# A two-layer encoder trunk: the order of a square, a sum, a root and a product in the last two token tiles of the gated recurrence

## The chip, the cores and the metric

The kernel runs on one core of one Trainium2 chip. The metric is the device time of one execution in microseconds (us); the time of a kernel is the median of its runs. The engines are named as in the profile: PE is TensorE (its weight loads are PEld), DVE is VectorE, ACT is ScalarE, POOL is GpSimd, SP issues most of the transfers. SBUF is the on-chip working memory, PSUM the eight banks that PE writes its products to.

## The reference, cut to what matters

Each of the two layers adds three branches to h: a mixer (latent attention, and two gated linear recurrences, GLA and HGRN2), a cross-attention on a memory, and a gated MLP. There are 512 tokens of 1024 numbers. The change lies in the end of the two recurrences:

```python
def gla_mixer(...):
    o = chunked_gated_recurrence(q * GLA_DK ** -0.5, k, v, log_alpha)   # 4 heads of 64
    o = rms_norm(o, out_norm) * jax.nn.silu(r)
def hgrn2_mixer(...):
    o = chunked_gated_recurrence(silu(q) * HGRN_DK ** -0.5, one_minus_f, i, log_f)
    o = rms_norm(o, out_norm) * jax.nn.silu(g)
...
h = h + jnp.concatenate([y_a, y_b, y_c], axis=-1) @ w_mix_out[l]
```

So for every token and head the 64 outputs are squared and summed, multiplied by the inverse root of their mean, then by a gate, and the 512 numbers of both recurrences go as columns 512 to 1023 into the product with `w_mix_out`.

## The kernel before, in words

The program is written by hand for each engine: every engine has its own instruction stream, runs it in the order in which it is written, and waits on semaphores (`wait_ge`, counted through `past(layer, ...)`). Nothing reorders it. Tokens are in NT = 4 tiles of 128, and the loop below is over them. Both layers run the same code.

The end of the recurrence, called here the tail, goes through five steps for each token tile n (numbered 0 to 3 as in the code; the third and the fourth tile are n = 2 and n = 3):

1. PE makes the outputs of the 8 heads in PSUM bank `O_BANKS[n]` = 2, 3, 0, 1 (lines 1169 and 1176), 128 tokens by 512 columns, and marks `o_mm`.
2. ACT squares the bank into `o_sq[:, n % 2]`, two buffers (line 1653).
3. DVE sums the squares by head (`squares`, line 2225, marks `o_ss`).
4. ACT takes the inverse root of the 8 means with a logarithm and an exponential (`inverse_rms`, lines 1378 and 1379, marks `o_r`), 128x8 numbers.
5. DVE multiplies the bank with the roots into `o_tok` in SBUF (`gated`, line 2231, marks `o_evac`): the root product.

Then comes the gate `sg_tok`. For tiles 0 to 2 POOL multiplies (`recurrences`, line 641, marks `o_done`), for tile 3 DVE does (line 2241, marks `last_o_done`); both inputs of these products, `o_tok` and `sg_tok`, lie in SBUF.

PE turns `o_tok` with 16 transposes into four banks (`turn_o`, line 1187). Their order is: tile 0 and 1 into banks 2 and 3 (4 transposes), tile 2 into banks 2 and 3, tiles 0 to 2 into bank 0, tiles 0 to 2 into bank 1 (8 that follow one behind the other), then tile 3 into banks 0, 1, 2, 3 (the last 4, which wait for `last_o_done`). Behind them on PE stand 6 matmuls of an operand that has long been there (`mix_units(MIX_UNITS["y"])`, with `ya_hi`, `ya_lo`), then the products with `yb_hi` and `yb_lo`, the two halves of the turned tiles, which ACT (line 1660) and DVE (line 2244) make out of the banks.

Weights come as slabs of 128x1024 numbers. Each is split into a rounded half `w_hi` (ACT, line 1370) and a rest `w_lo` (POOL, line 690: `raw` minus `w_hi`, both inputs in SBUF, one output to SBUF). POOL's stream has the tail's three gate products between the rest of slab ("mix", 0, 1) and that of ("mix", 0, 2): line 690 follows the gate product of tile 2 directly, it waits only for its `w_hi`, and its slab is the one that the first products with `yb_hi` use.

```python
POOL: for n in range(NT - 1): wait o_evac >= n + 1; o_tok[:, n] *= sg_tok[:, n]     # L641
      then, of the next slab:  wait hi_split;  w_lo = raw - w_hi                       # L690
DVE:  after gated(NT - 1):     wait sg_scaled, o_evac; o_tok[:, NT-1] *= sg_tok[:, NT-1]   # L2241
```

Of the kernel before, what the change touches and what calls it, by code (L numbers as in the profile page):

```python
# [27 lines left out]
def build_trunk(nc, A, out):  # L28
# [15 lines left out]
    NT, KD, MT = SEQ // P, D // P, NM // P  # L44
# [5 lines left out]
    GDK, GDV = A["gla_w_gate"].shape[2] // NH, A["gla_out_norm"].shape[1]  # L50
# [154 lines left out]
    for g in range(len(LG)):  # L205
        for c in range(LG[g]):
            ffn_in_slabs(g, c, LG_FIRST[g] + c)
        for q, (_, b) in enumerate(PRODUCTS):
            for s, nk in pair_slabs(g):
                slab(("out", g, q, s), nk, HALF, (b, g, s))  # L210
# [3 lines left out]
    def slab_of(layer, name):  # L214
        return layer * NS + slab_at[name]
# [9 lines left out]
    for gi, (_, _, src) in enumerate(flat):  # L225
        if callable(src):
            ring_of[gi] = len(in_ring)
            in_ring.append(gi)
        if gi in dma_los:
            continue  # L230
        if callable(src) and gi not in border:
            pool_los[gi] = len(pool_los) + 1
        else:
            out_los[gi] = len(out_los) + 1
# [9 lines left out]
    with ExitStack() as ctx:  # L244

        def sb(name, shape, dt=f32):
            return ctx.enter_context(nc.sbuf_tensor(name, shape, dt))
# [22 lines left out]
        small = sb("small", [P, 636])  # L270
# [112 lines left out]
        S = {n: ctx.enter_context(nc.semaphore(n)) for n in names}  # L383
# [38 lines left out]
        R_QK, R_O, R_KR = 260, 420, 548  # L422
# [53 lines left out]
        def past(layer, name):  # L476

            return layer * PER_LAYER[name]
# [15 lines left out]
        with nc.Block() as block:  # L494
# [833 lines left out]
            def _(act_):  # L1328
# [20 lines left out]
                for layer in range(DEPTH):  # L1349
                    def split_through(i):  # L1350

                        while nsplit[0] <= min(i, len(flat) - 1):
                            k = nsplit[0]
                            nk, cols, src = flat[k]
                            n = nk * cols
                            if k in ring_of:
                                whole = raw[ring_of[k] % RAW][:, 0:n]
                                act_.wait_ge(raw_in[ring_of[k] % RAW], arrivals[k])
                            else:
                                name, g, s = src  # L1360
                                whole = b_slab(k // NS, name, s, nk)
                                if name in T_AT:
                                    act_.wait_ge(S["t_done"], t_count(k // NS, g, name, s))
                                else:
                                    act_.wait_ge(b_in[name], b_loads(k // NS, g))
                            if k >= SPLIT:
                                act_.wait_ge(*released[k - SPLIT])
                            if k in dma_los:
                                act_.activation(w_lo[k % SPLIT][:, 0:n], whole, ACT.Copy, scale=-1.0).then_inc(S["negated"], 1)  # L1369
                            act_.activation(w_hi[k % SPLIT][:, 0:n], whole, ACT.Copy).then_inc(S["hi_split"], 1)  # L1370
                            nsplit[0] += 1

                    def ahead(name):

                        split_through(slab_of(layer, name) + SPLIT - 1)

                    def inverse_rms(dst, tmp, ss, n, done):
                        link(act_.activation(tmp, ss, ACT.Ln, bias=eps_c[:, 0:1], scale=1.0 / n))
                        act_.activation(dst, tmp, ACT.Exp, scale=-0.5).then_inc(done, 1)
# [83 lines left out]
                    if layer == 0:  # L1463
                        c = FIRST_K * P
# [77 lines left out]
                    for t in range(NT):  # L1542
                        c = R_QK + 4 * t
# [3 lines left out]
                    for t in range(NT):  # L1547
# [6 lines left out]
                        c = R_QK + 4 * (NT + t)  # L1554
# [90 lines left out]
                        act_.activation(k_hat[:, f, 0:NT - 1], pb[f][:, 0:(NT - 1) * P].rearrange("p (n q) -> p n q", n=NT - 1), ACT.Copy).then_inc(S["khat_evac"], 1)  # L1645
                    act_.preload_act_table_set(LOG_EXP)
                    ahead(("mix", 0, 1))
                    for n in range(NT + 1):
                        if n < NT:
                            act_.wait_ge(S["o_mm"], past(layer, "o_mm") + n + 1)  # L1650
                            if n > 1:
                                act_.wait_ge(S["o_ss"], past(layer, "o_ss") + n - 1)
                            act_.activation(o_sq[:, n % 2, :], pb[O_BANKS[n]][:, :], ACT.Square).then_inc(S["o_sq_done"], 1)
                        if n:
                            c = R_O + 8 * (n - 1)
                            act_.wait_ge(S["o_ss"], past(layer, "o_ss") + n)
                            inverse_rms(small[:, c + 64:c + 72], small[:, c + 32:c + 40], small[:, c:c + 8], GDV, S["o_r"])
                    for c in range(4):
                        act_.wait_ge(S["yT_mm"], past(layer, "yT_mm") + c + 1)
                        act_.activation(yb_hi[:, c, :], pb[c][:, :], ACT.Copy).then_inc(S["yT_hi"], 1)  # L1660
# [45 lines left out]
                    for t in range(NT):  # L1706
                        c = R_CQ + 4 * t
# [40 lines left out]
                    for g in range(len(LG)):  # L1748
                        for c in range(LG[g]):
                            n = LG_FIRST[g] + c  # L1750
# [28 lines left out]
            def _(dve):  # L1779
# [50 lines left out]
                for layer in range(DEPTH):  # L1830
# [377 lines left out]
                    for n in range(NT - 1):  # L2208
# [4 lines left out]
                        if n:  # L2213
                            for f in range(3):
                                c = slice(0, 256) if f == 0 else slice(P + f * P, 2 * P + f * P)
# [7 lines left out]
                    def squares(n):  # L2223
                        dve.wait_ge(S["o_sq_done"], past(layer, "o_sq_done") + n + 1)
                        dve.reduce_sum(small[:, R_O + 8 * n:R_O + 8 * n + 8], o_sq[:, n % 2, :].rearrange("p (h x) -> p h x", x=64), AX.X
                                       ).then_inc(S["o_ss"], 1)

                    def gated(n):
                        c = R_O + 8 * n + 64
                        dve.wait_ge(S["o_r"], past(layer, "o_r") + n + 1)  # L2230
                        dve.tensor_tensor(o_tok[:, n, :].rearrange("p (h x) -> p h x", x=64), pb[O_BANKS[n]][:, :].rearrange("p (h x) -> p h x", x=64),
                                          small[:, c:c + 8].unsqueeze(2).to_broadcast([P, 8, 64]), ALU.mult).then_inc(S["o_evac"], 1)

                    squares(0)
                    for n in range(NT):
                        if n + 1 < NT:
                            squares(n + 1)
                        gated(n)
                    dve.wait_ge(S["sg_scaled"], past(layer, "sg_scaled") + NT)
                    dve.wait_ge(S["o_evac"], past(layer, "o_evac") + NT)  # L2240
                    dve.tensor_tensor(o_tok[:, NT - 1, :], o_tok[:, NT - 1, :], sg_tok[:, NT - 1, :], ALU.mult).then_inc(S["last_o_done"], 1)  # L2241
# [22 lines left out]
                    for t in range(NT):  # L2264
                        c = R_CQ + 4 * t
# [34 lines left out]
                    for g in range(len(LG)):  # L2300
# [6 lines left out]
                        for c in range(LG[g]):  # L2307
                            n = LG_FIRST[g] + c
# [33 lines left out]
```

## Time and profile before

| what | value |
|---|---|
| median of 3 runs | 1375.46 us (1374.12 to 1375.72) |
| the profiled execution's own time | 1374.74 us |
| its span (first to last instruction) | 1373.0 us |
| mean granted TensorE clock | 1.000 |
| busy: PE, PEld, DVE, ACT, POOL | 99%, 82%, 70%, 51%, 38% |
| the tail of the first layer | about 206 to 219 us of the span |
| the tail of the second layer | about 886 to 900 us |

The span is the part of the execution that the profile shows; 1.74 us lie around it. Times within it count from its first instruction. A busy share is an average over the whole span; what a change in the tail is worth is read from the tail, by what each engine waits for there.

### The profile page before, as it was taken

What the parts mean: (1) busy time and instruction counts of PE and PEld (TensorE: products, weight loads), DVE (VectorE), ACT (ScalarE), POOL (GpSimd) and SP (SyncE); (2) the same over time, 40 slices, a digit from 0 to 9 for tenths busy, and PEclk for the clock granted to TensorE, in tenths of its full rate; (3) what the DMA queues carried; (4) which work ended last, traced back from release to release, by engine and by line L of the source; (5) the groups of instructions that cost most, each with busy time, mean ns of one, the idle gap of its engine ahead of it and who ended that gap; (6) DMA issues with size and microseconds to landing.
All of it is one profiled execution on the core that took longest, in us unless ns stands there. A gap on an engine that the chain in (4) does not pass through costs nothing.

```text
span 1373.0 us, 19396 instructions
## 1 busy us (share of the span) xinstructions
PE 1357.8 (99%) x7551; PEld 1128.6 (82%) x7551; DVE 958.8 (70%) x1380; ACT 705.6 (51%) x1170; POOL 516.0 (38%) x327
## 2 busy tenths in 40 slices
PE   8999999999999999999999999999999999999999
PEld 6888778887879988998988887788778888888887
DVE  4583773665889569857985657836658895797587
ACT  6747483665444344434466465835754433434333
POOL 5745665642430222032036456655335203220420
PEclk9999999999999999999999999999999999999999
DMA  6332112331471475066133220133325706741641
GB/s 181 100 91 74 31 47 79 122 108 49 150 200 47 144 194 138 17 177 154 22 92 93 86 77 16 48 97 118 92 62 169 198 17 177 191 107 39 189 95 61
DMA packets 180923, 142.58 MB, mean 104 GB/s; under 512 B 15169, under 2 KB 153184, under 8 KB 180832
## 3 DMA queue, kind: packets, MB, share of 16 engines
q1 hardware_dynamic: 175664, 124.55, 30.3%
q0 software_dynamic: 4608, 16.78, 6.4%
q8 instruction: 60, 0.98, 0.3%
q14 instruction: 31, 0.25, 0.1%
q10 hardware_dynamic: 560, 0.01, 0.0%
HBM read 122.44 MB, written 2.10 MB: 91 GB/s over the span
## 4 chain that ended last, share of the span: by engine, by line
PE 92%; DVE 4%; ACT 2%; DMA 1%; issue 1%; POOL 0%; SPq 0%; DVEq 0%; POOLq 0%
PE bank L770 27%; PE bank L772 27%; PE bank L771 27%; PE bank L944 2%; PE bank L1101 1%; PE bank L1102 1%; PE bank L1087 1%; PE bank L932 1%; DMA w_lo<-raw 1%; PE bank L1254 1%; PE bank L1169 1%; DVE scores_h L2181 1%; DMA x_tok<-in_x 1%; PE bank L1011 1%; DVE Q L2164 0%
## 5 line engine op out<-in xcount | busy, mean ns | idle before, releaser
L690 POOL TENSOR_TENSOR w_lo<-raw,w_hi 128x1024 fp32r<-128x1024 f32 (+3 forms) x148 | 360.0, 2437 | 642.0 <-ACT w_hi L1370 640.4
L770 PE MATMUL bank<-x_hi,w_hi 128*128 128x512 f32 x944 | 371.8, 394 | 4.0 <-DMA w_lo<-raw 1.9
L771 PE MATMUL bank<-x_lo,w_hi 128*128 128x512 f32 x944 | 367.7, 390 | 0.0
L772 PE MATMUL bank<-x_hi,w_lo 128*128 128x512 f32 x944 | 367.7, 389 | 0.0
L1370 ACT ACTIVATE w_hi<-raw 128x1024 fp32r<-128x1024 f32 (+2 forms) x181 | 189.4, 1047 | 125.5 <-PE bank L772 124.8
L770 PEld LDWEIGHTS bank<-x_hi,w_hi 128*128 128x128 f32 x944 | 177.2, 188 | 47.5 <-issue 8.0
L771 PEld LDWEIGHTS bank<-x_lo,w_hi 128*128 128x128 f32 x944 | 177.3, 188 | 37.2 <-issue 1.4
L772 PEld LDWEIGHTS bank<-x_hi,w_lo 128*128 128x128 f32 x944 | 177.2, 188 | 37.0
L771 PE MATMUL bank<-p_lo,w_hi 128*128 128x256 f32 x308 | 87.3, 283 | 0.0
L772 PE MATMUL bank<-p_hi,w_lo 128*128 128x256 f32 x308 | 87.3, 283 | 0.0
L770 PE MATMUL bank<-p_hi,w_hi 128*128 128x256 f32 x308 | 87.2, 283 | 0.0
L1729 ACT ACTIVATE conv<-conv 128x512 f32<-128x512 f32 x44 | 27.9, 633 | 113.8 <-DVE conv L2292 113.8
L770 PE MATMUL bank<-w_hi,x_hi 128*128 128x512 f32 (+1 forms) x192 | 77.3, 403 | 0.0
L772 PE MATMUL bank<-w_hi,x_lo 128*128 128x512 f32 (+1 forms) x192 | 74.0, 385 | 0.0
L771 PE MATMUL bank<-w_lo,x_hi 128*128 128x512 f32 (+1 forms) x192 | 73.8, 384 | 0.0
L1833 DVE SCALAR_TENSOR_TENSOR x_lo<-h,gains_all,x_hi 128x512 fp32r<-128x512 f32 x40 | 39.7, 1015 | 45.6 <-ACT x_hi L1390 44.8
L680 POOL DMA_DIRECT2D w_lo<-raw x32 | 28.8, 900 | 98.6 <-ACT w_lo L1369 98.6
L1369 ACT ACTIVATE w_lo<-raw 128x1024 fp32r<-128x1024 f32 x32 | 33.7, 1054 | 59.8 <-PE bank L772 59.8
L2296 DVE TENSOR_TENSOR act<-bank,r_bc 128x512 f32<-128x512 f32 x44 | 30.3, 688 | 42.9 <-PE bank L772 42.7
L770 PE MATMUL bank<-w_hi,p_hi 128*128 128x512 f32 x154 | 60.1, 390 | 0.0
L772 PE MATMUL bank<-w_hi,p_lo 128*128 128x512 f32 x154 | 60.0, 389 | 0.0
L771 PE MATMUL bank<-w_lo,p_hi 128*128 128x512 f32 x154 | 59.9, 389 | 0.0
(351 smaller groups left out, 2766.0 us busy)
## 6 DMA issues: line engine op xcount, KB each, us to landing
raw<-in_w_ffn_in SPq DMA_DIRECT2D x88, 512.0 KB, 4.2
w_lo<-raw POOLq DMA_DIRECT2D x32, 512.0 KB, 4.8
raw<-in_w_in SPq DMA_DIRECT2D x27, 512.0 KB, 3.8
raw<-in_w_mix_out SPq DMA_DIRECT2D x16, 512.0 KB, 3.9
raw<-in_w_ca_kv SPq DMA_DIRECT2D x32, 256.0 KB, 3.4
b_y<-in_w_ffn_out SPq DMA_DIRECT2D x10, 512.0 KB, 5.8
b_x<-in_w_ffn_out SPq DMA_DIRECT2D x10, 512.0 KB, 5.3
b_z<-in_w_ffn_out SPq DMA_DIRECT2D x10, 512.0 KB, 5.5
```

What stands on the lines that cost most here:

```text
L680: pool.dma_start(w_lo[gi % SPLIT][:, 0:n], raw[ring_of[gi] % RAW][:, 0:n], accum_op=ALU.add).then_inc(lo_in[dma_los[gi][0]], 16)
L690: pool.tensor_tensor(w_lo[gi % SPLIT][:, c0:n], whole[:, c0:n], w_hi[gi % SPLIT][:, c0:n].bitcast(f32), ALU.subtract).then_inc(S["lo_split ...
L770: pe.matmul(o, ah, bh, start=first, stop=False, skip_group_check=shared_bank)
L771: pe.matmul(o, ah, bl, start=False, stop=False, skip_group_check=shared_bank)
L772: mm = pe.matmul(o, al, bh, start=False, stop=last, skip_group_check=shared_bank)
L932: mm = pe.transpose(pb[b][:, c:c + P], pr[j % FLIGHT][:, c:c + P], ident[:, :])
L944: mm = pe.matmul(pb[b][:, q0:SEQ], values(n, hd), pT[hd % len(pT)][:, n, q0:SEQ], start=(n == 0), stop=(n == n_blocks - 1))
L1369: act_.activation(w_lo[k % SPLIT][:, 0:n], whole, ACT.Copy, scale=-1.0).then_inc(S["negated"], 1)
L1370: act_.activation(w_hi[k % SPLIT][:, 0:n], whole, ACT.Copy).then_inc(S["hi_split"], 1)
L1729: act_.activation(conv[n % 2][:, :], conv[n % 2][:, :], ACT.Silu).then_inc(S["silu_done"], 1)
L1833: dve.scalar_tensor_tensor(x_lo[:, k, :], h[:, k, :], gain_of(layer + w // 3, name, k), x_hi[:, k, :].bitcast(f32), ALU.mult, ALU.subtract ...
L2296: link(dve.tensor_tensor(act[n % 2][:, :], pb[b + 1][:, :], r_bc[:, :], ALU.mult))
```

## The change

In each layer ACT takes the roots of tile 2 before it squares tile 3, and DVE makes the root product of tile 2 before it sums the squares of tile 3. No instruction is added or removed, and no semaphore changes; PE, POOL and SP keep their order.

```diff
+                    def output_roots(n):
+                        c = R_O + 8 * n
+                        act_.wait_ge(S["o_ss"], past(layer, "o_ss") + n + 1)
+                        inverse_rms(small[:, c + 64:c + 72], small[:, c + 32:c + 40], small[:, c:c + 8], GDV, S["o_r"])
+
                     for n in range(NT + 1):
+                        if n == NT - 1:
+                            output_roots(n - 1)
                         if n < NT:
                             act_.wait_ge(S["o_mm"], past(layer, "o_mm") + n + 1)
                             if n > 1:
                                 act_.wait_ge(S["o_ss"], past(layer, "o_ss") + n - 1)
                             act_.activation(o_sq[:, n % 2, :], pb[O_BANKS[n]][:, :], ACT.Square).then_inc(S["o_sq_done"], 1)
-                        if n:
-                            c = R_O + 8 * (n - 1)
-                            act_.wait_ge(S["o_ss"], past(layer, "o_ss") + n)
-                            inverse_rms(small[:, c + 64:c + 72], small[:, c + 32:c + 40], small[:, c:c + 8], GDV, S["o_r"])
+                        if n and n != NT - 1:
+                            output_roots(n - 1)
...
                     squares(0)
-                    for n in range(NT):
-                        if n + 1 < NT:
-                            squares(n + 1)
+                    for n in range(NT - 2):
+                        squares(n + 1)
                         gated(n)
+                    gated(NT - 2)
+                    squares(NT - 1)
+                    gated(NT - 1)
```

ACT in the tail of the first layer, before. `o_sq` from bank0 is the square of tile 2, from bank1 that of tile 3; each pair L1378, L1379 is the roots of one tile, here of tiles 1, 2 and 3.

```order
L1653 ACTIVATE o_sq_91<-bank0 128x512
L1378 ACTIVATE small<-small,eps_c 128x8
L1379 ACTIVATE small<-small 128x8
L1653 ACTIVATE o_sq_91<-bank1 128x512
L1378 ACTIVATE small<-small,eps_c 128x8
L1379 ACTIVATE small<-small 128x8
L1378 ACTIVATE small<-small,eps_c 128x8
L1379 ACTIVATE small<-small 128x8
```

The same stretch of ACT in the changed kernel, where line 1653 has become 1660:

```order
L1660 ACTIVATE o_sq_91<-bank0 128x512
L1378 ACTIVATE small<-small,eps_c 128x8
L1379 ACTIVATE small<-small 128x8
L1378 ACTIVATE small<-small,eps_c 128x8
L1379 ACTIVATE small<-small 128x8
L1660 ACTIVATE o_sq_91<-bank1 128x512
L1378 ACTIVATE small<-small,eps_c 128x8
L1379 ACTIVATE small<-small 128x8
```

The square of tile 3 now stands behind the roots of tile 2 instead of ahead of them.

DVE in the same tail, before. The TENSOR_REDUCE of `o_sq` is the sum of one tile (the last one that of tile 3), `o_tok<-bank0` is the root product of tile 2, `o_tok<-bank1` that of tile 3, and the last row the gate product of tile 3:

```order
L2231 TENSOR_TENSOR o_tok_88<-bank3,small 128x512
L2225 TENSOR_REDUCE small<-o_sq_91 128x8
L2231 TENSOR_TENSOR o_tok_88<-bank0,small 128x512
L2231 TENSOR_TENSOR o_tok_88<-bank1,small 128x512
L2241 TENSOR_TENSOR o_tok_88<-o_tok_88,sg_tok_99 128x512
```

And in the changed kernel, where lines 2225, 2231 and 2241 have become 2230, 2236 and 2248:

```order
L2236 TENSOR_TENSOR o_tok_88<-bank3,small 128x512
L2236 TENSOR_TENSOR o_tok_88<-bank0,small 128x512
L2230 TENSOR_REDUCE small<-o_sq_91 128x8
L2236 TENSOR_TENSOR o_tok_88<-bank1,small 128x512
L2248 TENSOR_TENSOR o_tok_88<-o_tok_88,sg_tok_99 128x512
```

The root product of tile 2 has moved ahead of the sum of tile 3; the gate product stays last.

## Rows read from the trace of the kernel before

**Rows 1.** The page, part 4: shares of the chain that ended last, by engine.

```profile
PE 92%; DVE 4%; ACT 2%; DMA 1%; issue 1%; POOL 0%; SPq 0%; DVEq 0%; POOLq 0%
```

**Rows 2.** Waits of PE, whole span: us in total, times, longest.

```profile
PE bank L1187 <- POOL o_tok L641: 1.4, 2, 0.7
```

**Rows 3.** Chain that ended last, 204 to 222 us: start us, us, what.

```profile
213.50 0.61 DVE o_tok L2231
...
214.25 1.28 POOL o_tok L641
```

**Rows 4.** DVE timeline, first layer's tail: start us, us, engine, line, what [idle before].

```profile
211.01 0.69 DVE L2225 TENSOR_REDUCE small<-o_sq 128x8 f32<-128x512 f32 x1 [0.25 <-ACT o_sq L1653]
...
212.82 0.69 DVE L2225 TENSOR_REDUCE small<-o_sq 128x8 f32<-128x512 f32 x1 [0.52 <-ACT o_sq L1653]
...
213.42 0.68 DVE L2231 TENSOR_TENSOR o_tok<-bank,small 128x512 f32<-128x512 f32 x1
...
214.11 0.69 DVE L2231 TENSOR_TENSOR o_tok<-bank,small 128x512 f32<-128x512 f32 x1
214.91 1.15 DVE L2241 TENSOR_TENSOR o_tok<-o_tok,sg_tok 128x512 f32<-128x512 f32 x1
```

**Rows 5.** POOL timeline, first layer's tail.

```profile
212.44 1.30 POOL L641 TENSOR_TENSOR o_tok<-o_tok,sg_tok 128x512 f32<-128x512 f32 x1 [0.26 <-DVE o_tok L2231]
214.25 1.27 POOL L641 TENSOR_TENSOR o_tok<-o_tok,sg_tok 128x512 f32<-128x512 f32 x1 [0.51 <-DVE o_tok L2231]
215.47 2.84 POOL L690 TENSOR_TENSOR w_lo<-raw,w_hi 128x1024 fp32r<-128x1024 f32 x1
```

**Rows 6.** ACT timeline, first layer's tail.

```profile
211.20 0.21 ACT L1379 ACTIVATE small<-small 128x8 f32<-128x8 f32 x1
212.19 0.60 ACT L1653 ACTIVATE o_sq<-bank 128x512 f32<-128x512 f32 x1 [0.78 <-PE bank L1176]
```

**Rows 7.** PE and PEld timelines, first layer's tail, several short stretches.

```profile
215.57 0.33 PE L1187 MATMUL bank<-ident,o_tok 128*128 128x128 f32 x1 [0.70 <-POOL o_tok L641]
...
216.50 0.60 PE L1187 MATMUL bank<-ident,o_tok 128*128 128x128 f32 x4
...
217.86 0.39 PE L771 MATMUL bank<-ya_lo,w_hi 128*128 128x512 f32 x1
218.09 0.40 PE L772 MATMUL bank<-ya_hi,w_lo 128*128 128x512 f32 x1
218.37 0.50 PE L770 MATMUL bank<-yb_hi,w_hi 128*128 128x512 f32 x1
218.70 0.40 PE L771 MATMUL bank<-yb_lo,w_hi 128*128 128x512 f32 x1
...
218.37 0.19 PEld L770 LDWEIGHTS bank<-yb_hi,w_hi 128*128 128x128 f32 x1 [0.32 <-POOL w_lo L690]
```

**Rows 8.** Second layer's tail: timelines of DVE and POOL.

```profile
891.58 0.69 DVE L2225 TENSOR_REDUCE small<-o_sq 128x8 f32<-128x512 f32 x1 [0.70 <-ACT o_sq L1653]
...
893.01 1.29 POOL L641 TENSOR_TENSOR o_tok<-o_tok,sg_tok 128x512 f32<-128x512 f32 x1 [0.71 <-DVE o_tok L2231]
...
895.47 1.15 DVE L2241 TENSOR_TENSOR o_tok<-o_tok,sg_tok 128x512 f32<-128x512 f32 x1
```

**Rows 9.** Instructions of lines 2298 and 690: duration ns min/median/max.

```profile
L2298 DVE TENSOR_TENSOR act<-conv,act x44: 691/692/695, 363.6 to 1341.7; 128x512 f32<-128x512 f32 x44
...
L690 POOL TENSOR_TENSOR w_lo<-raw,w_hi x148: 1292/2402/3403, 12.4 to 1320.7; 128x1024 fp32r<-128x1024 f32 x135, 128x928 fp32r<-128x928 f32 x8, 128x768 fp32r<-128x768 f32 x4, 128x512 fp32r<-128x512 f32 x1
```

**Rows 10.** POOL and DVE timelines elsewhere, where their two-input products meet.

```profile
241.65 2.40 POOL L690 TENSOR_TENSOR w_lo<-raw,w_hi 128x1024 fp32r<-128x1024 f32 x1 [3.04 <-ACT w_hi L1370]
...
242.23 2.38 DVE L1833 SCALAR_TENSOR_TENSOR x_lo<-h,gains_all,x_hi 128x512 fp32r<-128x512 f32 x1 [13.32 <-ACT x_hi L1390]
...
61.10 0.63 DVE L2070 TENSOR_TENSOR r_diag<-q_tok,rot_tab 128x128 f32<-128x128 f32 x1
61.12 0.47 POOL L705 TENSOR_TENSOR rot_tab<-sin,spread 128x128 f32<-128x128 f32 x1
```

## The prediction, made before the changed kernel ran

> **What bounds the kernel now.** I read the page first: the chain that ended last lies to 92% on PE [rows 1]. So the end moves by what PE loses or wins in waiting, and by nothing else. Second, the waits of PE: in the tail of each layer it stands 0.7 us before a transpose (L1187) until POOL has made the gate product of tile 2 (L641), 1.4 us in all [rows 2]. Third, the chain through the first layer's tail, where the reader sees why POOL is late: the root product of tile 2 on DVE (213.50 on the chain, recorded from 213.42) hands to POOL at 214.25, and POOL to PE at 215.57 [rows 3, 7]. Fourth, DVE's timeline [rows 4]: that root product starts only when DVE is done with the sum of tile 3 (212.82, next start 213.42), and this sum waited for a square that ACT began at 212.19 [rows 6]. The roots of tile 2 need only the sum of tile 2, done at 211.01 + 0.69 = 211.70. That wait is what the change goes at. Last, POOL's timeline [rows 5], for what comes behind the gate products: a weight rest L690, at once.
>
> **Step 1, ACT.** Two activations move ahead of one; none is added. The roots of a tile take 0.60 us from the end of its sum to the start of its root product (212.82 + 0.69 = 213.51 to 214.11 [rows 4]). So the roots of tile 2 run from 211.70 to 212.30, the moved exponential ending about 212.27. ACT is idle there now: its exponential of tile 1 ends at 211.41, the square of tile 3 starts at 212.19 [rows 6]. The square may start 0 to 0.1 us later; it ends at 212.79 to 212.9. Price 0, since DVE does not want it before 212.90 (step 2).
>
> **Step 2, DVE.** Root product of tile 2 at 212.30 instead of 213.42: 1.12 us earlier. The sum of tile 3 stands behind it, and a DVE instruction that waits for nothing starts 0.60 after the one ahead (212.82 to 213.42): 212.90, 0.08 later than now. Then 0.69 for the sum, 0.60 for the roots of tile 3, 0.69 for its root product, and the 0.11 that separate that product from L2241 now (214.80 to 214.91): L2241, tile 3's gate product, starts at 212.90 + 0.69 + 0.60 + 0.69 + 0.11 = 214.99 instead of 214.91.
>
> **Step 3, POOL.** The product of tile 1 ends at 212.44 + 1.30 = 213.74 [rows 5]. That of tile 2 no longer waits for DVE, and POOL starts a ready instruction some 0.05 before the end of the one ahead (215.52 against 215.47): 213.69, ending at 213.69 + 1.27 = 214.96, which is 0.56 earlier than 215.52. Behind it L690, whose only wait was long satisfied, starts at 214.91 instead of 215.47.
>
> **Step 4, who is late next.** Without more, PE would get tile 2 at 215.01 (0.05 after POOL, as now) and win. But L2241 and L690 now arrive almost together, L690 ahead by 0.08 us, and the trace shows that such two do not run together. L2241 takes 1.15 us now [rows 4], while another DVE product of the same size with both inputs in SBUF takes 0.69 in all 44 cases [rows 9]. It ends at 216.06, 0.54 after the POOL product under which it began (215.52); and L690, recorded from 215.47, takes 2.84 against a median of 2.40 [rows 5, 9]: each waited for the other in turn. The full price is seen at 241.65: L690 runs 2.40 to 244.05, and a DVE product that starts at 242.23 takes 2.38, ending 0.56 past it [rows 10]. The order is by who is there first: L2241 had stood for 0.56 us when L690 came, so it went next.
>
> In the changed kernel L690 is first. It runs from 214.91 to 217.31; L2241, from 214.99, ends 0.55 later at 217.86 instead of 216.06. PE's last 4 transposes wait for that. The 8 ahead of them start at 215.01 and are issued by about 215.95, so PE idles about 2 us. The last four start now at 216.50, with no wait; then at 217.86 + 0.05 = 217.91, and the first one behind a wait takes 0.33 instead of 0.27 [rows 7], 0.06 more. PE's loss: 217.97 - 216.50 = **1.47 us**. The yb halves, the products behind them and everything later are made from these transposes and shift along.
>
> One small gain stands against it. The first yb product waits now for the rest that L690 makes (215.47 + 2.84 = 218.31; its weight load at 218.37 is put down to POOL). Its two steps, 218.09 to 218.70, take 0.61 instead of twice 0.23 (217.86 to 218.09) [rows 7]. In the changed kernel that rest is there at 217.31 and PE comes 1.47 later: 0.15 us goes away. Bounds: 0 (if the yb half takes over as the one waited for) to 0.15; I take 0.15, since POOL is the one named.
>
> The second layer gives the same [rows 8]: roots of tile 2 from 892.27, L2241 at 892.27 + 0.60 + 0.60 + 0.69 + 0.60 + 0.69 + 0.11 = 895.56 against 895.47 now; POOL's tile 2 at 893.01 + 1.29 - 0.05 = 894.25, L690 at 894.25 + 1.27 - 0.05 = 895.47, first by 0.09.
>
> **Sum.** 2 x (1.47 - 0.15) = +2.64 us. PE's work behind it waits for data that PE's own results set off, so nothing gives the time back. The profiled execution took 1374.74, so 1377.38; the median of the runs is 0.72 above it, which gives **1378.1 us**, 0.19% more. With the small gain at 0, and L690 0.1 longer or shorter, the sum lies between 2.4 and 3.1; with the runs' own spread of 0.8 to either side the likeliest case spans 1377.2 to 1379.2.
>
> **The order of two that meet, against the notes.** A row shows how near a meeting can be: L2070 on DVE is recorded from 61.10, POOL's L705 from 61.12, directly behind another L705; L2070 still ended 0.14 past the end of that POOL product [rows 10], so POOL kept its turn though recorded 0.02 later. The Trainium skill (SBUF — State Buffer, section "SBUF: two separate sides") says that GpSimd and a VectorE instruction with two SBUF inputs share one port pair, which whichever starts first holds for its whole instruction while the other fully blocks. By that rule the sum is the same 2.64, as L690 starts first, with 0.08 to spare; the row disagrees with it by 0.02 in POOL's favour, and the row decides, so there is 0.1 to spare.
>
> **Rivals.**
> - *L2241 goes first, or nothing blocks it* (the one on the other side: not slower). It decides if L2241 comes ahead of L690 by more than 0.02, so if my sums are off by 0.1: POOL's tile 2 0.1 longer, or DVE's sum of tile 3 sooner. Then L2241 takes 0.69, from 214.99 to 215.68; PE's first of 8 transposes starts at 215.02 and its ninth 0.93 behind, at 215.95, against 216.50: 0.55 won. L690 would be done at 215.68 + 2.25 = 217.93 (now 218.31, 2.25 after L2241's end), which PE, by then 0.55 early, would await some 0.1 longer. About 0.45 won twice: 1374.6. For it: 0.08 us is little. Against it: five of the durations in the sum repeat within 0.01 in the second layer, and L2070. Chance 0.10.
> - *One layer each way*: +1.32 - 0.45, 1376.3. The two layers differ by 0.01 in the sums, so 0.05.
> - *The change does little*: the square of tile 3 is delayed by what the roots of tile 2 gain, or POOL takes up its next product as late as now. Then L690 and L2241 meet as now: 1375.5. Against it: ACT's idle 0.78 ahead of that square [rows 6]. Chance 0.07.
> - *Two rests go ahead of L2241*, L690 being followed by another L690: 2.36 more per layer, 1382.8. Against it: the turn about in rows 4 and 5, where the one that stood waiting went next. Chance 0.05.
>
> **How the numbers follow.** The forecast has 0.73. A measurement of this kernel tells a difference from none at about 0.2%, 2.75 us. The likeliest sum of 2.64 lies just under it, its upper part above: of the 0.73 I give 0.30 to slower and 0.43 to no difference. With 0.05 from the two rests slower has 0.35; no difference has 0.43 + 0.10 + 0.05 + 0.07 less 0.02 for a larger win, 0.63; faster 0.02. The range runs from 1375.4 to 1379.2: the likeliest case, the mixed one and most of the one that does little; left out are the case of L2241 first, the two rests and tails, under 2 in 10.
>
> **What the profile of the changed kernel would show.** Step 1 and 2 right: the root product of tile 2 starts about 0.60 behind the sum of tile 2 in both tails, the sum of tile 3 right behind it, the last gate product 0.08 later than now. Step 3: POOL's third gate product starts without idle time. Step 4: the last gate product takes about 2.9 us instead of 1.15, L690 about 2.40 instead of 2.84, and PE's wait at the transposes is put down to DVE, near 2 us twice, instead of to POOL, 0.7. The prediction is wrong if that gate product takes 0.7 to 1.2 us; then the time falls by a microsecond or stays.

## The result, and the profile after

| kernel | median | runs | ratio to the kernel before, 95% interval |
|---|---|---|---|
| before | 1374.85 us (1372.83 to 1376.97) | 12 | 1 |
| changed | 1377.79 us (1377.36 to 1379.74) | 12 | 1.0026, 1.0018 to 1.0034 |
| changed, measured once more beside 21 runs of before (1375.13) | 1377.73 us (1377.04 to 1380.08) | 11 | 1.0022, 1.0013 to 1.0031 |

The change costs 2.6 to 2.9 us by the medians, 3.0 to 3.6 by the ratios. The third line is the run `after_again`, told below with the experiments. The profiled execution took 1377.56 us, its span is 1375.9 us. The share of the chain on PE is the same 92% as in [rows 1]:

```profile
PE 92%; DVE 4%; ACT 2%; DMA 1%; issue 1%; POOL 0%; DVEq 0%
```

What PE waits for in the tails is not. Where it stood 0.7 us twice for POOL [rows 2], the view of PE's waits (us in total, times, longest) now has two lines:

```profile
PE bank L1187 <- DVE o_tok L2248: 3.5, 2, 1.8
...
PE bank L1187 <- POOL o_tok L641: 0.6, 2, 0.4
```

Both halves of the change are seen there: POOL is earlier by more than half of its wait, and a new, longer wait for DVE has taken its place. DVE's timeline in the first tail, which answers to [rows 4] (line 2236 is the root product, 2230 the sum, 2248 the gate product of tile 3):

```profile
212.28 0.69 DVE L2236 TENSOR_TENSOR o_tok<-bank,small 128x512 f32<-128x512 f32 x1
212.88 0.67 DVE L2230 TENSOR_REDUCE small<-o_sq 128x8 f32<-128x512 f32 x1
...
214.17 0.69 DVE L2236 TENSOR_TENSOR o_tok<-bank,small 128x512 f32<-128x512 f32 x1 [0.61 <-ACT small L1379]
214.96 2.88 DVE L2248 TENSOR_TENSOR o_tok<-o_tok,sg_tok 128x512 f32<-128x512 f32 x1
...
897.12 2.84 DVE L2248 TENSOR_TENSOR o_tok<-o_tok,sg_tok 128x512 f32<-128x512 f32 x1
```

The root product of tile 2 starts at 212.28 instead of 213.42, and the three steps behind it follow as before. The gate product comes at 214.96, 0.05 later than before, and takes 2.88 us instead of 1.15; the last line is the same instruction in the second tail. POOL's timeline, which answers to [rows 5], shows what it is held by:

```profile
213.70 1.29 POOL L641 TENSOR_TENSOR o_tok<-o_tok,sg_tok 128x512 f32<-128x512 f32 x1
214.94 2.36 POOL L690 TENSOR_TENSOR w_lo<-raw,w_hi 128x1024 fp32r<-128x1024 f32 x1
...
217.25 2.83 POOL L690 TENSOR_TENSOR w_lo<-raw,w_hi 128x1024 fp32r<-128x1024 f32 x1
...
897.06 2.34 POOL L690 TENSOR_TENSOR w_lo<-raw,w_hi 128x1024 fp32r<-128x1024 f32 x1
```

POOL's product of tile 2 follows its product of tile 1 without idle time, 0.55 us earlier than before, and so does the weight rest: 214.94, ahead of the gate product by 0.02 us (0.06 in the second tail). The rest runs undisturbed to 214.94 + 2.36 = 217.30; the gate product ends at 214.96 + 2.88 = 217.84, 0.54 behind it. The next rest, taken up at 217.25, is the one that now pays: 2.83, as the first one did before. PE's timeline, two instants of each tail:

```profile
215.04 0.33 PE L1187 MATMUL bank<-ident,o_tok 128*128 128x128 f32 x1 [0.42 <-POOL o_tok L641]
...
217.90 0.33 PE L1187 MATMUL bank<-ident,o_tok 128*128 128x128 f32 x1 [1.76 <-DVE o_tok L2248]
...
897.16 0.33 PE L1187 MATMUL bank<-ident,o_tok 128*128 128x128 f32 x1 [0.17 <-POOL o_tok L641]
...
900.01 0.55 PE L1187 MATMUL bank<-ident,o_tok 128*128 128x128 f32 x3 [1.76 <-DVE o_tok L2248]
```

The eight transposes that wait for POOL's tile 2 start at 215.04, where [rows 7] have 215.57; the last four, which started at 216.50, now start at 217.90. These are instants of two executions, though, and PE comes to this tail 0.23 us sooner in the second one. Counted from PE's first matmul with `ya_hi` in the tail (shown next), the last four start 1.63 later than before in the first tail (6.05 instead of 4.42) and 1.39 later in the second (5.81 instead of 4.42). The first of the four takes 0.06 more.

To compare the tails of many kernels I measure one length in each: from the start of PE's first matmul with `ya_hi` behind the recurrence (the same instruction in every kernel) to the start of the first addition to h on DVE. In the kernel before it is 15.53 and 15.46 us (212.08 to 227.61, 892.64 to 908.10), from the timelines of PE and DVE:

```profile
212.08 0.50 PE L770 MATMUL bank<-ya_hi,w_hi 128*128 128x512 f32 x1
...
892.64 0.50 PE L770 MATMUL bank<-ya_hi,w_hi 128*128 128x512 f32 x1
```

```profile
227.61 0.69 DVE L1900 TENSOR_TENSOR h<-h,bank 128x512 f32<-128x512 f32 x1 [7.68 <-PE bank L772]
...
908.10 0.69 DVE L1900 TENSOR_TENSOR h<-h,bank 128x512 f32<-128x512 f32 x1 [7.62 <-PE bank L772]
```

The same lines of the changed kernel:

```profile
211.85 0.50 PE L770 MATMUL bank<-ya_hi,w_hi 128*128 128x512 f32 x1
...
894.20 0.50 PE L770 MATMUL bank<-ya_hi,w_hi 128*128 128x512 f32 x1
```

```profile
230.48 0.69 DVE L1905 TENSOR_TENSOR h<-h,bank 128x512 f32<-128x512 f32 x1 [9.10 <-PE bank L772]
...
910.97 0.69 DVE L1905 TENSOR_TENSOR h<-h,bank 128x512 f32<-128x512 f32 x1 [7.48 <-PE bank L772]
```

So 18.63 and 16.77: longer by 3.10 and by 1.31. The second is the loss that the wait explains (1.39 and 0.06, less the small gain behind the weight rest). The first has two things more. One is when PE comes, read from DVE's sum of tile 2:

```profile
210.99 0.68 DVE L2230 TENSOR_REDUCE small<-o_sq 128x8 f32<-128x512 f32 x1
...
893.14 0.69 DVE L2230 TENSOR_REDUCE small<-o_sq 128x8 f32<-128x512 f32 x1
```

PE's first `ya_hi` matmul starts 0.86 us behind that sum in the first tail and 1.06 behind it in the second; in the kernel before it was 1.07 and 1.06 ([rows 4, 8]). So in the first tail PE arrives 0.2 us sooner at a wait that ends no sooner. Every tail of a kernel with both halves of the change, in the experiments too, has one of these two values (0.85 to 0.86, or 1.06 to 1.07), and in a profile that has both, the tail with the smaller value is 0.2 to 0.25 us the longer one by this measure, the clock aside.

The other thing is the clock, which the view by stretches shows (us, busy PE, PEld, DVE, ACT, POOL with counts, granted clock, DMA share, GB/s):

```profile
216.00:218.00 2.00, 0.24 (x3) 0.10 (x2) 1.84 (x1) 0.00 (x0) 2.00 (x2) 1.00 0.00 0
218.00:219.00 1.00, 1.00 (x6) 0.91 (x7) 0.10 (x1) 0.73 (x2) 1.00 (x1) 0.70 0.36 72
219.00:220.00 1.00, 1.00 (x4) 0.81 (x3) 1.00 (x2) 1.00 (x3) 1.00 (x1) 0.50 0.91 322
220.00:221.00 1.00, 1.00 (x4) 0.72 (x4) 1.00 (x3) 0.33 (x1) 0.08 (x1) 0.50 0.40 148
221.00:222.00 1.00, 1.00 (x4) 0.81 (x3) 0.38 (x1) 0.73 (x1) 0.00 (x0) 0.60 0.51 131
222.00:223.00 1.00, 1.00 (x6) 0.80 (x6) 0.00 (x0) 0.33 (x1) 0.59 (x1) 1.00 0.90 322
...
900.00:901.00 1.00, 0.99 (x7) 0.90 (x8) 0.00 (x0) 0.62 (x2) 1.00 (x1) 1.00 0.34 41
```

Behind the idle 1.76 us PE ran at the lower of its two clocks, 1.2 instead of 2.4 GHz, for some 3 us of the first tail; a 128x512 matmul there takes 0.63 instead of 0.39. Behind the second tail's gap the clock stayed at 1.00. In `after_again` a tail with the value 0.85 and no fall of the clock is 1.57 longer than before, so the fall itself costs 3.10 - 1.57 = 1.5 us. The two tails are 4.41 longer together and the span only 2.9: elsewhere this execution waited less than the one profiled before (PE's waits for the `w_lo` transfers 1.0 instead of 1.9, its pauses put down to "issue" at line 1169 0.2 instead of 1.0, against 0.3 more for `x_tok`), and such pauses differ between any two profiles.

### The profile page after: what moved, and what is told of

Same layout as the page of the kernel before. It is cut to its first block, busy times and chain, and to the rows that moved or that the text cites. A ratio compares the mean times of both kernels' runs of the same rounds, so it can differ in the third digit from the quotient of the medians.

```text
span 1375.9 us, 19396 instructions
## 1 busy us (share of the span) xinstructions
PE 1359.4 (99%) x7551; PEld 1129.5 (82%) x7551; DVE 962.5 (70%) x1380; ACT 705.4 (51%) x1170; POOL 515.9 (37%) x327
## 4 chain that ended last, share of the span: by engine, by line
PE 92%; DVE 4%; ACT 2%; DMA 1%; issue 1%; POOL 0%; DVEq 0%
PE bank L770 27%; PE bank L772 27%; PE bank L771 27%; PE bank L944 2%; PE bank L1101 1%; PE bank L1102 1%; PE bank L1087 1%; PE bank L932 1%; PE bank L1254 1%; DVE scores_h L2186 1%; DMA w_lo<-raw 1%; PE bank L1011 1%; PE bank L778 0%; DVE Q L2169 0%; PE bank L1055 0%
```

## The experiments

The theory under test (the port theory of the expectations): the gate product on DVE and the weight rest on POOL, both with two inputs from SBUF, do not run at once; who comes first goes first, and the new order lets POOL come first. Each tail's length is given beside the kernel before's 15.53 and 15.46; the waits and durations are from each run's own profile.

| run | median | ratio to before, 95% interval | tails, longer by | gate product of tile 3 |
|---|---|---|---|---|
| `pool_pause` | 1374.70 | 1.0001, 0.9992 to 1.0009 | -0.38, -0.16 | 0.69, 0.69 |
| `act_half` | 1375.58 | 1.0006, 0.9997 to 1.0014 | +0.02, +0.02 | 1.15, 1.15 |
| `dve_half` | 1379.83 | 1.0042, 1.0029 to 1.0056 | +1.72, +3.23 | 2.27, 2.27 |
| `pe_filled` | 1377.83 | 1.0020, 1.0012 to 1.0029 | +1.35, +1.58 | 2.84, 2.89 |
| `gate_in_psum` | 1373.50 | 0.9993, 0.9984 to 1.0001 | -0.65, -0.42 | none |
| `old_order_psum` | 1374.34 | 0.9999, 0.9990 to 1.0007 | -0.14, -0.12 | none |
| `two_in_psum` | 1372.90 | 0.9989, 0.9980 to 0.9998 | -0.58, -0.39 | none |
| `rest_in_halves` | 1375.15 | 1.0003, 0.9994 to 1.0012 | +0.26, +0.27 | 1.78, 1.76 |
| `after_again` | 1377.73 | 1.0022, 1.0013 to 1.0031 | +1.33, +1.57 | 2.84, 2.87 |

The first four ran beside 27 runs of before (median 1374.54), the next three beside 27 (1374.38), the last two beside 21 (1375.13). `dve_half` has 5 runs of its own, the others 11.

### A pause on POOL ahead of the weight rest

```diff
+        spare = sb("spare", [P, 128])
...
                     pool.tensor_tensor(o_tok[:, n, :], o_tok[:, n, :], sg_tok[:, n, :], ALU.mult).then_inc(S["o_done"], 1)
+                pool.memset(spare[:, :], 0.0)
```

> The changed kernel, with a memset of 128x128 on POOL (no input) between its gate product of tile 2 and the weight rest behind it, 0.1 to 0.2 us of added work. Port theory (the last gate product on DVE and the weight rest on POOL cannot read SBUF two inputs at a time, and who comes first goes first): the rest now comes 0.1 us after the gate product instead of 0.03 to 0.06 before it, so the gate product takes 0.70 to 0.75 us instead of 2.88, the rest about 2.9 instead of 2.36, PE waits under 0.2 us for tile 3, and the kernel falls by some 3.5 us to 0.4 to 1.1 us under the kernel before. Rival (the new order itself, or the later sum of tile 3, costs the 2.9 us): the gate product stays at 2.9 us, or the time stays 2.5 to 3.5 us above the kernel before.

Measured: the timelines of DVE and of POOL in the first tail (the rest has become line 692):

```profile
214.91 0.69 DVE L2250 TENSOR_TENSOR o_tok<-o_tok,sg_tok 128x512 f32<-128x512 f32 x1
```

```profile
214.83 0.22 POOL L643 MEMSET spare<- 128x128 f32 x1
214.99 2.86 POOL L692 TENSOR_TENSOR w_lo<-raw,w_hi 128x1024 fp32r<-128x1024 f32 x1
```

The added work puts the rest 0.08 behind the gate product (0.12 in the second tail), and the roles change: the gate product is not held at all, the rest takes 2.86. PE has no wait for DVE in the tails any more. The two tails are 0.54 us shorter than in the kernel before, the lower half of what was expected; the median, expected 0.4 to 1.1 under the kernel before, is 0.2 above it and the same within the interval, and 3 us under the changed kernel. One instruction of 0.22 us more on POOL, and the loss is gone: the order of arrival makes it, not the new order of the tiles as such.

### ScalarE's part alone

```diff
                     for n in range(NT + 1):
+                        if n == NT - 1:
+                            output_roots(n - 1)
...
-                        if n:
...
+                        if n and n != NT - 1:
+                            output_roots(n - 1)
```

> Only ScalarE's part of the change: roots of tile 2 ahead of the square of tile 3, VectorE in the old order. Port theory: nothing that POOL or PE waits for moves. The root product of tile 2 still stands behind the sum of tile 3, the last gate product still comes 0.56 us ahead of the weight rest and takes 1.15 us; time equal to the kernel before within 0.5 us. Rival (the square of tile 3 is late behind the roots): sum of tile 3 later by 0.1 to 0.3 us, time up by as much twice, up to 0.6 us. Rival (ScalarE's order carries the loss): 2 to 3 us above.

Measured: both tails within 0.02 us of the kernel before, with PE's wait unchanged:

```profile
PE bank L1187 <- POOL o_tok L641: 1.4, 2, 0.7
```

The median is 1.0 us higher where at most 0.5 was expected, with an interval that takes in no change. ScalarE's part by itself moves nothing in the tail, and the square of tile 3 is not late.

### VectorE's part alone

```diff
                     squares(0)
-                    for n in range(NT):
-                        if n + 1 < NT:
-                            squares(n + 1)
+                    for n in range(NT - 2):
+                        squares(n + 1)
                         gated(n)
+                    gated(NT - 2)
+                    squares(NT - 1)
+                    gated(NT - 1)
```

> Only VectorE's part of the change, ScalarE in the old order (square of tile 3, then roots of tile 2). Port theory: the root product of tile 2 now waits for roots that come 0.9 us later than in the changed kernel, and the sum of tile 3 stands behind it, so the last gate product comes at about 215.93 in the first layer, some 0.6 us after the start of the weight rest (215.29), and is held to its end: it ends near 218.24 instead of 216.06. PE loses 1.85 - 0.15 = 1.7 us per layer, 3.4 in all, more where the clock falls behind the gap of PE: 1378 to 1381, slower than the whole change by 0.5 or more. Rival (the two halves add up, each half carrying a part of the 2.9): between the kernel before and the changed one.

Measured, the timelines of DVE and of POOL in the first tail:

```profile
215.79 2.27 DVE L2243 TENSOR_TENSOR o_tok<-o_tok,sg_tok 128x512 f32<-128x512 f32 x1
```

```profile
215.17 2.35 POOL L690 TENSOR_TENSOR w_lo<-raw,w_hi 128x1024 fp32r<-128x1024 f32 x1
```

The gate product comes 0.62 after the start of the rest and ends at 218.06, 0.54 behind the rest's end (217.52): the held product ends a fixed time behind what holds it, whenever it comes. The first tail is 1.72 longer (1.7 was expected); behind the second the clock fell again (0.50 from 900 to 903 us), and it is 3.23 longer. The kernel is 5.3 us slower than before by the medians, and 2.0 slower than the whole change, as only the theory had it; with 5 runs the two ratio intervals still overlap. The tails say the same with less noise: 1.72 where the whole change has 1.31 to 1.57 without a fall of the clock; and 3.23 - 1.72 gives the fall the same 1.5 us as above. VectorE's half is the part that costs, and ScalarE's half takes some of it back.

### The weight rest in two halves

```diff
+                        if i == slab_at["mix", 0, 2]:
+                            pool.tensor_tensor(w_lo[gi % SPLIT][:, c0:n // 2], whole[:, c0:n // 2],
+                                               w_hi[gi % SPLIT][:, c0:n // 2].bitcast(f32), ALU.subtract)
+                            c0 = n // 2
                         pool.tensor_tensor(w_lo[gi % SPLIT][:, c0:n], whole[:, c0:n],
```

> The changed kernel, but the weight rest that stands behind POOL's gate products is made in two instructions of 512 columns instead of one of 1024; same values, same order. Port theory (the gate product on VectorE is held for the one POOL instruction that came before it, and goes ahead of the next): the first half takes some 1.25 to 1.3 us instead of 2.36, the gate product 1.75 to 1.85 instead of 2.88, PE's wait for tile 3 falls from 1.8 to 0.7 us in each tail, and the loss from 1.31 to about 0.25 us per tail: 0.3 to 0.8 above the kernel before, and no fall of the clock behind the tail. Rival (POOL keeps the port as long as it has work queued): gate product still 2.9 us or more, 2.6 to 2.9 us above. Rival (the price does not depend on what POOL does): the same.

Measured, the timelines of DVE and of POOL in the first tail, and PE's waits:

```profile
216.28 1.78 DVE L2252 TENSOR_TENSOR o_tok<-o_tok,sg_tok 128x512 f32<-128x512 f32 x1
```

```profile
216.23 1.28 POOL L691 TENSOR_TENSOR w_lo<-raw,w_hi 128x512 fp32r<-128x512 f32 x1
```

```profile
PE bank L1191 <- DVE o_tok L2252: 1.4, 2, 0.7
```

The gate product is held for the one instruction of 1.28 us that came before it and goes ahead of the second half, though POOL has that queued. Its hold shrinks with the half, and the loss per tail with it, from 1.31 to 0.26 (0.25 was expected). The median, expected 0.3 to 0.8 above the kernel before, is the same as its median within the interval, which reaches 1.0012. So the port is handed over between instructions, and the length of one POOL instruction is the price.

### The gate of tile 3 in its PSUM bank, new order and old

In both kernels PE's last four transposes wait for `o_evac` instead of `last_o_done`, and the gate product of SBUF with SBUF is replaced by one of PSUM with SBUF, ahead of the root product:

```diff
+                    def gate_in_bank(n):
+                        dve.wait_ge(S["sg_scaled"], past(layer, "sg_scaled") + n + 1)
+                        link(dve.tensor_tensor(pb[O_BANKS[n]][:, :], pb[O_BANKS[n]][:, :], sg_tok[:, n, :], ALU.mult))
...
                     squares(NT - 1)
+                    gate_in_bank(NT - 1)
                     gated(NT - 1)
...
-                    dve.tensor_tensor(o_tok[:, NT - 1, :], o_tok[:, NT - 1, :], sg_tok[:, NT - 1, :], ALU.mult).then_inc(S["last_o_done"], 1)
```

`old_order_psum` has the same with the kernel before's order around it.

> The changed kernel, but tile 3's gate is multiplied into its PSUM bank while the roots are being made (one input from PSUM, one from SBUF), and the root product comes last; no product on VectorE in the tail has two SBUF inputs, and the separate gate product of 0.7 us is gone from the chain. Port theory: nothing holds anything, the weight rest starts at the end of POOL's third product and takes 2.40, PE does not wait for tile 3, only for POOL's tile 2 (some 0.2 us), so the last four transposes start 0.55 us earlier than in the kernel before and the 0.15 behind the weight rest goes too: 0.70 us per tail, 1.4 in all, 1373.1 (faster by 0.1%). Rival (the new order has a cost of its own): at or above the kernel before.

> The kernel before with the same gate in the PSUM bank for tile 3, in the old order of ScalarE and VectorE. Port theory: POOL's product of tile 2 starts as late as before and PE waits 0.7 us for it as before; the only gain is that the weight rest takes 2.40 instead of 2.84, 0.15 us per tail, 0.3 in all: 1374.2, the same. So the change of order is worth 1.1 us once nothing is held by the port. Rival (the gate product on VectorE was itself what PE waited for, and the order is worth nothing): the same time as with the new order, 1.4 us under the kernel before.

Measured with the new order, DVE and POOL in the first tail, and PE's waits:

```profile
214.88 0.69 DVE L2241 TENSOR_TENSOR bank<-bank,sg_tok 128x512 f32<-128x512 f32 x1
215.64 0.69 DVE L2236 TENSOR_TENSOR o_tok<-bank,small 128x512 f32<-128x512 f32 x1
```

```profile
216.31 2.38 POOL L690 TENSOR_TENSOR w_lo<-raw,w_hi 128x1024 fp32r<-128x1024 f32 x1
```

```profile
PE bank L1187 <- POOL o_tok L641: 0.6, 2, 0.4
```

And PE's waits with the old order:

```profile
PE bank L1187 <- POOL o_tok L641: 1.4, 2, 0.7
```

The gate in PSUM takes 0.69 while POOL's product of tile 2 runs beside it (it started at 215.06), and the rest takes 2.38: with one SBUF input on DVE nothing is held. In the old order PE still waits 1.4 us for POOL and the tails gain 0.26 together, the part behind the weight rest (0.3 was expected). In the new order PE waits 0.6 us and the tails gain 1.07 (1.4 was expected): 0.65 in the tail where PE waits 0.17 (0.70 was expected), and 0.42 in the one where PE comes 0.2 us sooner (the smaller of the two values) and waits 0.40. So the order that cost 2.6 us is worth some 0.8 once the two engines do not meet. By the medians the kernel is 0.9 us faster than before; the interval just takes in no change.

### The gates of tiles 2 and 3 in PSUM

```diff
-                for n in range(NT - 1):
+                for n in range(NT - 2):
                     pool.wait_ge(S["sg_scaled"], past(layer, "sg_scaled") + n + 1)
...
+                    gate_in_bank(NT - 2)
                     gated(NT - 2)
                     squares(NT - 1)
+                    gate_in_bank(NT - 1)
                     gated(NT - 1)
```

> The new order with the gates of tiles 2 and 3 multiplied in their PSUM banks on VectorE; POOL makes only those of tiles 0 and 1. Port theory and the chain: tile 2 is ready on VectorE at about 213.55 of the first tail instead of 215.0 on POOL, PE turns the first 12 without a wait, and the last four start at about 215.53 (VectorE, four more 0.6 us steps) instead of 216.50: 0.9 us per tail and 0.15 behind the weight rest, 2.1 in all: 1372.4 (faster by 0.15%). Rival (VectorE, with one more product in the chain, becomes the bound): the last four wait until 216 or later, and the gain is no larger than with tile 3 alone, 1.4 us.

Measured: PE's waits.

```profile
PE bank L1187 <- DVE o_tok L2236: 0.7, 2, 0.4
```

And PE's timeline in the first tail, the transposes behind that wait:

```profile
216.92 0.98 PE L1187 MATMUL bank<-ident,o_tok 128*128 128x128 f32 x7 [0.24 <-DVE o_tok L2236]
```

The rival held: with one product more in its chain VectorE is what PE waits for, and the two tails are 0.97 shorter than before, no more than with tile 3 alone (1.07). The median is the lowest of all, 1372.90, 0.11% under before with an interval that ends below 1. The wait comes one step ahead of where the rival put it: seven transposes stand behind it, the three of tiles 0 to 2 into bank 1 and the last four. Bank 1 holds the outputs of tile 3 until their root product has read them, so that product's place in VectorE's chain counts for these three as well. That the median beats `gate_in_psum` is not shown, since their intervals overlap and their tails do not differ that way.

### The gap of PE filled, and the changed kernel once more

`pe_filled` adds 16 transposes of the identity ahead of the last four; `after_again` is the changed kernel itself.

```diff
+                    for _ in range(16):
+                        pe.transpose(pb[0][:, (NT - 1) * P:NT * P], ident[:, :], ident[:, :])
                     for c in range(4):
                         mark(turn_o(NT - 1, c), S["yT_mm"])
```

> The changed kernel with 16 added transposes of the identity on PE ahead of the last four, 16 x 0.109 = 1.74 us of work in the 2 us for which PE stands idle; they write columns that the last four overwrite. Clock theory (after the gap of 2 us PE runs at half the clock for 3 us in some tails, 1.55 us lost each time): the granted clock stays at 1.00 in every run, the gate product still takes 2.9 us, the median lies 0 to 1 us under the changed kernel's, and the runs that lay 1 to 2 us above its lowest are gone. Rival (the spread of the changed kernel's runs has another cause): clock 0.998 or 0.999 in some runs and single runs 1.5 us above the lowest, as before.

> The changed kernel itself, another profile of it. Port theory: gate product 2.8 to 2.9 us in both tails and PE waiting 1.8 us for it each time, whatever the clock does; 2.6 to 3.5 us above the kernel before. Clock: of the two tails none, one or both are followed by some 3 us at half the clock; where one is not, the tail is 1.3 us longer than in the kernel before, where it is, about 3. Rival (the fall of the clock in the first profile was bound to the first layer): it falls there again and not in the second.

Measured with the gap filled, the first tail by stretches:

```profile
216.00:218.00 2.00, 1.98 (x19) 1.74 (x18) 1.75 (x1) 0.00 (x0) 2.00 (x2) 1.00 0.03 8
218.00:219.00 1.00, 1.00 (x8) 0.87 (x7) 0.20 (x1) 0.83 (x2) 1.00 (x1) 1.00 0.49 90
219.00:220.00 1.00, 1.00 (x6) 0.72 (x5) 1.00 (x2) 1.00 (x3) 1.00 (x1) 1.00 1.00 348
```

And the changed kernel's second profile, the wait and the stretch behind it:

```profile
PE bank L1187 <- DVE o_tok L2248: 3.5, 2, 1.8
```

```profile
222.00:223.00 1.00, 1.00 (x7) 0.82 (x6) 0.48 (x1) 1.00 (x3) 1.00 (x1) 1.00 0.66 180
```

Its second tail, from which the price of a fall was taken above, has its sum of tile 2, its first `ya_hi` matmul and its first addition to h at these instants (timelines of DVE, PE and DVE):

```profile
895.57 0.68 DVE L2230 TENSOR_REDUCE small<-o_sq 128x8 f32<-128x512 f32 x1
```

```profile
896.42 0.50 PE L770 MATMUL bank<-ya_hi,w_hi 128*128 128x512 f32 x1
```

```profile
913.45 0.69 DVE L1905 TENSOR_TENSOR h<-h,bank 128x512 f32<-128x512 f32 x1 [7.50 <-PE bank L772]
```

In `pe_filled` PE is busy 1.98 of 2 us in the gap and the clock stays at 1.00 in both tails, but the expectation missed: 5 of its 11 executions still have a mean clock of 0.999, and its median and highest run are those of the changed kernel. In `after_again` PE stands idle for the same 1.8 us twice and the clock falls in neither tail; the tails are 1.33 and 1.57 longer. So in these profiles a tail of the changed order is 1.3 to 1.6 us longer without a fall of the clock and about 1.5 more with one, and a fall came behind 2 of the 6 gaps of 1.8 us that were left idle (the changed kernel's first tail, `dve_half`'s second).

Whether the gap causes falls in the runs without a profile is left open, and their mean clock cannot tell. The kernel before, which has no gap of that length in its tails, is below 1.000 in 5 and in 8 of the 27 runs of the first two groups and in none of the 21 beside `after_again`; `pool_pause`, where the gap is gone, is below it in 5 of 11. The profiles of `gate_in_psum` and `old_order_psum`, both of executions with 0.999, show one reason: PE's timeline and the stretches of `gate_in_psum`, near the start of the span:

```profile
12.50 0.62 PE L770 MATMUL bank<-x_hi,w_hi 128*128 128x512 f32 x1 [1.43 <-DVE x_lo L2037]
```

```profile
13.00:14.00 1.00, 1.00 (x5) 0.70 (x4) 0.83 (x3) 0.73 (x2) 0.93 (x1) 0.50 1.31 255
```

There the clock fell behind another idle stretch of PE, of 1.43 us, which the kernel before has too (1.42, with the clock at 1.00 in its profile), and stayed at 1.00 in the tails. A filled gap in the tail could not have brought such runs to zero.

## Why the prediction was right, point by point

- **The bound and step 1.** The roots of tile 2 moved ahead, and the square did not cost anything; `act_half` shows both tails unmoved.
- **Step 2.** The root product of tile 2 was put at 212.30 and came at 212.28, the sum of tile 3 at 212.90 and came at 212.88. The gate product was put at 214.99 and came at 214.96. That the instants agree so well is luck: PE was 0.23 sooner in this execution, and DVE's sum of tile 2 happened to start at 210.99, beside 211.01 before. What the step forecast is the way from that sum to the gate product, 3.98 us, and it took 3.97 and 3.98 in the two tails.
- **Step 3.** POOL's product of tile 2 was put at 213.69 (came at 213.70), the weight rest at 214.91 (214.94), with the same luck. From the one to the other 1.22 was forecast; it was 1.23 to 1.24.
- **Step 4.** The lead of the rest over the gate product was put at 0.08 us. It was 0.02 and 0.06, and between 0.02 and 0.06 in every profile of this order: right in sign, with less to spare than the sums had it. The gate product was expected to take 2.9 us, the rest 2.40; they took 2.88 and 2.36. PE's loss was put at 1.47 and the small gain at 0.15, 1.32 per tail: the tails without a fall of the clock lost 1.31, 1.33 and, where PE came 0.2 us sooner, 1.57. The experiments that take the meeting away (`pool_pause`, `gate_in_psum`) or halve it (`rest_in_halves`) move the time as this step has it.
- **The rule on the port.** The Trainium skill (SBUF — State Buffer, section "SBUF: two separate sides") gives GpSimd and a VectorE instruction with two SBUF inputs one shared port pair, which the one that starts first holds for its whole instruction. The runs agree: 2.88 us held by a rest of 2.36, 1.78 by a half of 1.28, 0.69 where VectorE was first or read one input from PSUM.
- **The sum.** +2.64 us was forecast, 1378.1 against a median of 1375.46; measured were +2.94 and, the second time, +2.60. The forecast and its range held. How near they came is in part luck: in the two profiles of the changed kernel the tails are 4.41 and 2.90 us longer in all, and the spans 2.9 and 5.4, so terms that the sum does not have are as large as the sum. For the same reason the profiles do not show that nothing behind the tails gives time back, as the prediction had it. The chances were less sharp: 0.63 went to no difference, 0.43 of it on the ground that 0.2% can hardly be told from none. The runs tell more than that: the intervals are 0.08 to 0.09% to either side, and both lie above 1, from 1.0018 and from 1.0013, so the change is slower.
- **What the steps left out.** The forecast had PE's gap of 2 us but no price for it beyond the wait; in some tails the clock falls behind it, which adds 1.5 us to that tail. It also took PE to come to every tail as it does in the kernel before; where PE comes 0.2 us sooner, the tail is that much longer.
- **The rivals.** That VectorE goes first is what `pool_pause` makes happen by 0.1 us; its tails gained 0.54 together, not the 0.9 that the rival's price had. That two rests go ahead was wrong: in every profile the gate product went next.

## What to carry to other kernels

When a step is moved up, look at what its engine does next: here POOL, set free half a microsecond earlier, took up a long instruction just before VectorE needed the port, and a product that had been held for the last 0.6 us of a POOL instruction was held for a whole one of 2.4. Two engines that share a resource by whole instructions make the price of a change jump at a lead of hundredths of a microsecond; take the resource out of the chain (one operand left in PSUM) or keep the instructions beside it short, rather than count on the order of arrival. A profile of before shows the danger already: a product that takes 1.15 us where its like takes 0.69 in all 44 cases.

## What the runs showed that was not expected

- Adding 0.22 us of work to POOL takes about 3 us off the changed kernel's median (1377.8 to 1374.7); by the work alone it would have cost time.
- A tail's length depends on when PE comes to it: 0.2 us sooner makes it 0.2 us longer, at one of two values, in every kernel with both halves of the change.
- The clock fell behind an idle stretch of PE of 1.8 us in 2 of 6 tails, to 0.50 for some 3 us, and not in the other four with the same stretch; in two other profiles it fell behind one of 1.43 us.
- The pauses of PE elsewhere differ between profiles by as much as this change is worth: before the outputs of the third tile (line 1169, "issue") they were 1.0, 0.2 and 1.1 us in all in the kernel before and the two profiles of the changed one.
